# Stick-breaking queries and keys projected right behind the values, their scores and chain beside the other projection units

## The chip, the cores and the metric

The kernel runs on one core of a Trainium2 chip. The metric is the device time of one execution, in microseconds (us). Engines: PE (TensorE, matmuls), DVE (VectorE), ACT (ScalarE), POOL (GpSimd), SP (SyncE, which issues the DMAs here).

## The reference

Two transformer-like blocks of two layers each work on 256 tokens of width 1024, in float32. The change touches the first block, which runs twice (layers 0 and 1). Cut to what matters:

```
h = rms(x, ln1) * (1 + sc1) + sh1
qa,ka,va,qi,ki,wi,qb,kb,vb,qc,kc,vc = split(h @ w_in)
oa = dsa(rope(rms(qa)), rope(rms(ka)), va, rope(qi), rope(ki), wi)    # index scores, top 64 keys of each query, softmax
ob = stick_breaking(qb, kb, vb)      # no norm, no rope: z = q.k/8, log-sigmoids, reverse cumulative sum, exp
oc = window_softmax(rope(rms(qc)), rope(rms(kc)), vc, sinks)          # 8 heads in two groups, c0 and c1
x += g1 * (rms([oa, ob, oc]) @ w_o)
x += g2 * swiglu(rms(x) ...)
```

There are four heads each in the groups a, b, c0 and c1. Queries come in two blocks of 128 (n = 0 with 128 keys, n = 1 with 256 keys), so a group is two tiles.

## The kernel before, in words

**Units.** Weights stream in as units of 128 output columns (two DMAs of 256 KB). Each float32 weight is split: ACT writes the high part WH (L2158), DVE the low part of the first half (L2419, `split_low`) and POOL that of the second half (L1763, `low`); a unit is then 24 matmuls (L1846 to L1848). Four units are in flight: behind unit x every engine prepares unit x + 4, and ACT may overwrite WH only when unit x is done. Each engine works through one fixed program order and meets the others by semaphores; nothing is reordered.

**The projection** has 20 units: 0 to 3 (index queries, index keys, one key of c), 4 to 7 (values, as two pairs), then 8 to 19. Before: 8 a key of c, 9 the key of a, 10 to 13 queries of c, 14 and 15 queries of a, 16 and 17 queries of b, 18 and 19 keys of b. ACT evicts each unit from PSUM into F (L2259; with gain and a square for the normed ones, L2252 and L2257). Beside the units, PE sums squares over heads (`key_sums` L1955, `query_sums` L1965), rotates for rope (`rotate` L1982, bank 4 of PSUM) and computes index scores. `rotate(r)` of r > 0 waits until DVE has read rotation r - 1 out of bank 4 (`rot_read`); rotations of keys also wait for `k_normed`, which DVE's `key_norm` gives (four instructions, L2434, L2436, L2440, L2586). DVE ends a rope with L2575 (reads bank 4) and L2578 (adds POOL's cosine part, L1756). DVE's `highest` (L2616, L2620) takes the next 8 maxima of the index scores; 8 of them and `select` (L2627, L2631) give the top 64.

**The attention stage** runs from the last unit to the output projection. For a tile, PE computes scores (`score`: mask L2049, scores L2053), DVE its maxima (`begin`, L2687), ACT the exponentials (`exps`, L2279); PE transposes the weights (`turn`, L2069), ACT copies them (`turned_copy`, L2308 for n = 0, L2311 for n = 1), PE multiplies by the values (`weigh`, L2081), and ACT takes the heads out (`heads_out`, L2321 and L2322). The tiles go in the order of TILES: c0 0, b 0, c0 1, b 1, c1 0, c1 1, a 0, a 1. The score of a 0 waits for `select`. The b tiles have a chain of their own: `stick_begin` (DVE L2666), `stick_logs` (ACT L2288, L2290, L2292), `stick_sums` (DVE L2674, four scans L2678, L2681), `stick_exps` (ACT L2297). In the attention stage PE also multiplies the conditioning vector by streamed weights (`modulate`, L1827, 1 MB of `mods` a step, a ring of two steps); steps 5 to 15 stand between the tiles. At the end PE transposes the outputs (L2113).

Of the kernel before, what the change touches and what calls it, by code (L numbers as in the profile page):

```python
# [46 lines left out]
KEY_I, VALUES, QUERY_C, QUERY_A = 2, 4, 10, 14  # L47
KEYS = (3, 8, 9)
GAIN_OF = {3: 7, 8: 7, 9: 2, **{QUERY_C + i: 3 for i in range(4)}, QUERY_A: 0, QUERY_A + 1: 0}
ROPES = ((0, 2), (2, 1), (3, 2), (6, 2), (8, 2), (5, 1), (10, 2))  # L50
KEY_ROPES = {2: 1, 5: 2}
HEADS = {"c0": (6, 3, 1, 4, 0), "c1": (8, 4, 2, 6, 64), "a": (10, 5, 0, 0, 128), "b": (12, 14, 3, 2, 256)}
# [90 lines left out]
def build(nc, stream, mods, consts, consts2, par1, par2, lam, ccols, xT, ctxT, outT):  # L143
# [1598 lines left out]
    def _(pool):  # L1742
# [63 lines left out]
    def _(pe):  # L1806
# [109 lines left out]
        def first_layer(l):  # L1916
# [29 lines left out]
            def key_sums(c):  # L1946

                for x in KEYS[2:] if c else KEYS[:2]:
                    evicted(pe, base + x)
                if c:  # L1950
                    pe.wait_ge(mr_done, 2 * l + 1)
                else:
                    pe.wait_ge(rot_read, 7 * l + 2)
                cut = slice(2, 3) if c else slice(0, 2)
                pe.matmul(PS[:, 4, 0:(2 - c) * T], heads, SQK[:, cut, :], start=True, stop=True).then_inc(ms_done, 1)  # L1955

            def query_sums(chunks):

                for x in chunks:
                    i = x - QUERY_A if x >= QUERY_A else x - QUERY_C + 2  # L1960
                    evicted(pe, base + x)
                    pe.wait_ge(index_read, 2 * l + 2)
# [7 lines left out]
            def rotate(r):  # L1970
# [9 lines left out]
                if r in (2, 3, 4):  # L1980
                    pe.wait_ge(mr_done, 2 * l + 2)
# [13 lines left out]

            steps = iter(range(at + (NORM_STEPS if l else 0), at + QK_STEPS))
            for x in range(IN_UNITS):
# [6 lines left out]
                if x == 2:  # L2004
                    if l == 0:
                        pe.wait_ge(consts_in, 16)
                    rotate(0)
                if x == 5:
                    rotate(1)
# [16 lines left out]

            def score(i):

                name, n = SCORED[i]
                w = P * (n + 1)  # L2030
                first, key = HEADS[name][:2]
                if i < 2:
                    for x in range(16, 20):
                        evicted(pe, base + x)
                elif i < 4:
                    pe.wait_ge(stick_read, 2 * l + i - 1)
                else:
                    pe.wait_ge(exped, 6 * l + i - 3)
                if name == "c0":
                    pe.wait_ge(rope_done, 7 * l + 4)  # L2040
                if name == "c1":
                    pe.wait_ge(rope_done, 7 * l + 5)
                if name == "a":
                    pe.wait_ge(rope_done, 7 * l + 7)
                    pe.wait_ge(sel_done, l + 1)
                if name != "b":
                    m = (SELB if name == "a" else BAND)[:, n, 0:w][:, None, :].broadcast_to([P, 2, w])
                    for half in range(2):
                        pe.matmul(banks(n)[:, 2 * half:2 * half + 2, 0:w], IDB, m, start=True, stop=False)  # L2049
                for p, h in enumerate(PLACE):  # L2050
                    r = slice(64 * (h % 2), 64 * (h % 2) + 64)
                    k = key + h // 2 if name == "b" else key
                    last = pe.matmul(banks(n)[:, p, 0:w], F[r, first + h // 2, n * P:(n + 1) * P], F[r, k, 0:w],  # L2053
                                     start=name == "b", stop=name == "b" or p % 2 == 1)
                last.then_inc(scores, 1)
# [94 lines left out]
    def _(act):  # L2150
# [82 lines left out]
        def first_layer(l):  # L2233
            base = l * PER
            norm(l, 0)
            def key_roots(c):

                cut, n = slice(2, 3) if c else slice(0, 2), 2 - c
# [3 lines left out]
                             (mr_done, 2 * l + c + 1), rx_done)  # L2242

            for x in range(IN_UNITS):
# [18 lines left out]
                if x == 11:  # L2263
                    key_roots(1)
            act.wait_ge(stats_done, l + 1)
# [18 lines left out]
            def stick_logs(n):  # L2284

# [729 lines left out]
```

## Time and profile before

| | |
|---|---|
| time, 3 runs | 2315.23, 2323.94, 2323.98 us; median 2323.94 |
| span of the profiled execution | 2314.6 us |
| granted TensorE clock, mean over the span | 0.986 |
| PE, DVE, ACT, POOL busy | 96%, 56%, 48%, 33% |
| DMA | 328.47 MB, mean 142 GB/s |

The times of the three runs don't say which of them was profiled; the span lies 0.6 us under the lowest of them and 9.3 us under the median. The mean shares run over stages with different limits, so the stages around the change are read by themselves. Times of rows are from the start of the span; a number in brackets is the engine's idle time before the row and what ended it.

### The profile page before, as it was taken

The page shows a single profiled execution, that of the slowest core. Times are in us where ns is not written, and L with a number is a line of the kernel's source. Part 1 is how long each engine was busy: PE and PEld are TensorE (multiplying, and loading weights), DVE is VectorE, ACT ScalarE, POOL GpSimd, SP SyncE. Part 2 cuts the span into 40 slices and gives each one's busy share as a digit, 9 for nine tenths or more (in the row PEclk, how much of TensorE's full clock was granted, in tenths as well). Part 3 has the DMA queues.
Part 4 walks back from the last instruction along what each step waited for, and adds up shares of the span by engine and source line. Part 5 has one row for each costly group of instructions (what it writes and reads, how often), then busy time and mean ns, then how long its engine had stood idle before and what let it go on. Part 6 is the DMA issues. An engine that isn't in the chain of part 4 may idle for free.

```text
span 2314.6 us, 41122 instructions
## 1 busy us (share of the span) xinstructions
PE 2220.9 (96%) x14780; PEld 1935.8 (84%) x14780; DVE 1304.0 (56%) x2274; ACT 1112.3 (48%) x2324; POOL 764.9 (33%) x563
## 2 busy tenths in 40 slices
PE   7989998989999899999999999999989999999998
PEld 4859997868999798878878679888879999787998
DVE  3668999666445725541253764364455564437663
ACT  3565554554555535532364653232343565647553
POOL 2405874513565221112222012222213235221443
PEclk9999999999999999999999999999999999999999
DMA  8766998667766331222222113222323335222554
GB/s 303 230 219 208 322 315 301 201 210 241 237 186 196 96 91 57 64 73 91 82 74 83 35 36 94 91 73 91 99 73 110 105 116 171 83 83 65 170 162 140
DMA packets 159781, 328.47 MB, mean 142 GB/s; under 512 B 17696, under 2 KB 21024, under 8 KB 159520
## 3 DMA queue, kind: packets, MB, share of 16 engines
q1 hardware_dynamic: 159504, 325.80, 43.8%
q8 instruction: 89, 1.46, 0.2%
q0 software_dynamic: 144, 0.85, 0.1%
q14 instruction: 44, 0.36, 0.0%
HBM read 325.53 MB, written 1.05 MB: 141 GB/s over the span
## 4 chain that ended last, share of the span: by engine, by line
PE 65%; issue 14%; DVE 9%; POOL 5%; DMA 2%; ACT 2%; SPq 1%; POOLq 0%; ACTq 0%; DVEq 0%
PE PS L1846 13%; PE PS L1847 13%; PE PS L1848 13%; PE PS L1891 4%; PE PS L1893 4%; PE PS L1892 4%; POOL WL L1763 4%; DVE WORK L2521 3%; DVE WL L2419 2%; PE PS L729 2%; PE PS L709 1%; DMA RAW<-stream 1%; POOL AR L1783 1%; PE PS L743 1%; DMA WORK<-mods 1%
## 5 line engine op out<-in xcount | busy, mean ns | idle before, releaser
L1763 POOL TENSOR_TENSOR WL<-RAW,WH 128x512 fp32r<-128x512 f32 x434 | 618.7, 1427 | 1447.9 <-ACT WH L2158 1298.0
L1846 PE MATMUL PS<-AR,WH 128*128 128x256 f32 (+1 forms) x2632 | 857.9, 326 | 3.4 <-DVE AR L1614 1.9
L1847 PE MATMUL PS<-AR,WH 128*128 128x256 f32 (+1 forms) x2632 | 844.1, 321 | 0.0
L1848 PE MATMUL PS<-AR,WL 128*128 128x256 f32 (+1 forms) x2632 | 844.0, 321 | 0.0
L2158 ACT ACTIVATE WH<-RAW 128x512 fp32r<-128x512 f32 x840 | 490.6, 626 | 302.5 <-PE PS L1848 190.6
L2419 DVE TENSOR_TENSOR WL<-RAW,WH 128x512 fp32r<-128x512 f32 x434 | 372.5, 858 | 448.9 <-ACT WH L2158 447.2
L1846 PEld LDWEIGHTS PS<-AR,WH 128*128 128x128 f32 x2632 | 496.8, 189 | 58.8 <-issue 12.1
L1847 PEld LDWEIGHTS PS<-AR,WH 128*128 128x128 f32 x2632 | 496.8, 189 | 41.4 <-issue 2.4
L1848 PEld LDWEIGHTS PS<-AR,WL 128*128 128x128 f32 x2632 | 496.5, 189 | 40.1
L1891 PE MATMUL PS<-WH,AR 128*128 128x256 f32 x768 | 219.2, 285 | 0.0
L1893 PE MATMUL PS<-WH,AR 128*128 128x256 f32 x768 | 216.3, 282 | 0.0
L1892 PE MATMUL PS<-WL,AR 128*128 128x256 f32 x768 | 216.3, 282 | 0.0
L1891 PEld LDWEIGHTS PS<-WH,AR 128*128 128x128 f32 x768 | 144.7, 188 | 3.3 <-issue 3.0
L1892 PEld LDWEIGHTS PS<-WL,AR 128*128 128x128 f32 x768 | 144.7, 188 | 0.7 <-issue 0.5
L1893 PEld LDWEIGHTS PS<-WH,AR 128*128 128x128 f32 x768 | 144.6, 188 | 0.0
L1908 PE MATMUL PS<-AR,WH 128*128 128x256 f32 x352 | 99.9, 284 | 2.7 <-DVE WL L2419 2.4
L1909 PE MATMUL PS<-AR,WH 128*128 128x256 f32 x352 | 99.1, 282 | 0.0
L1910 PE MATMUL PS<-AR,WL 128*128 128x256 f32 x352 | 99.1, 282 | 0.0
L2521 DVE SCALAR_TENSOR_TENSOR WORK<-WORK 128x1024 f32<-128x1024 f32 x48 | 88.9, 1852 | 0.0
L1030 ACT ACTIVATE WORK<-PS 128x512 f32<-128x512 f32 (+1 forms) x48 | 23.5, 490 | 125.6 <-PE PS L1848 125.5
L1092 ACT ACTIVATE WORK<-PS,BC,QN 128x512 f32<-128x512 f32 (+1 forms) x96 | 66.9, 705 | 8.9 <-DVE BC L1490 8.8
L1488 DVE TENSOR_REDUCE BC<-PS 128x2 f32<-128x1024 f32 (+1 forms) x48 | 50.1, 1044 | 36.0 <-PE PS L709 36.0
(310 smaller groups left out, 3103.0 us busy)
## 6 DMA issues: line engine op xcount, KB each, us to landing
RAW<-stream SPq DMA_DIRECT2D x868, 256.0 KB, 3.0
WORK<-mods SPq DMA_DIRECT2D x144, 512.0 KB, 5.8
WORK<-stream SPq DMA_DIRECT2D x68, 256.0 KB, 4.7
C<-consts SPq DMA_DIRECT2D x1, 1088.0 KB, 7.4
XX<-xT SPq DMA_DIRECT2D x1, 1024.0 KB, 9.8
XX<-ctxT SPq DMA_DIRECT2D x1, 1024.0 KB, 7.7
outT<-XX SPq DMA_DIRECT2D x1, 1024.0 KB, 4.8
C<-consts POOLq DMA_DIRECT2D x1, 832.0 KB, 7.0
```

What stands on the lines that cost most here:

```text
L1763: pool.tensor_tensor(WL[:, u % 4, cut, :], raw(u, 1), WH[:, u % 4, cut, :].bitcast(f32), ALU.subtract).then_inc(lo_done[1], 1)
L1846: pe.matmul(out, WH[:, u % 4, k, :], moving[:, 0, k, :], start=(k == 0), stop=False)
L1847: pe.matmul(out, WH[:, u % 4, k, :], moving[:, 1, k, :], start=False, stop=False)
L1848: last = pe.matmul(out, WL[:, u % 4, k, :], moving[:, 0, k, :], start=False, stop=(k == KC - 1))
L1891: pe.matmul(out, still[:, 0, k, cut], WH[:, both, k, :], start=(k == 0), stop=False)
L1892: pe.matmul(out, still[:, 0, k, cut], WL[:, both, k, :], start=False, stop=False)
L1893: last = pe.matmul(out, still[:, 1, k, cut], WH[:, both, k, :], start=False, stop=(k == KC - 1))
L1908: pe.matmul(PS[:, b, 0:T], WH[:, u % 4, k, :], HID[:, 0, kk, :], start=(kk == 0), stop=False)
L1909: pe.matmul(PS[:, b, 0:T], WH[:, u % 4, k, :], HID[:, 1, kk, :], start=False, stop=False)
L2158: act.activation(WH[:, u % 4, cut, :], raw(u, half), ACT.Copy).then_inc(hi_done, 1)
L2419: dve.tensor_tensor(WL[:, u % 4, cut, :], raw(u, 0), WH[:, u % 4, cut, :].bitcast(f32), ALU.subtract).then_inc(lo_done[0], 1)
L2521: dve.scalar_tensor_tensor(UNREAD, GFLAT[:, h % 4, :], 1.0, CB, ALU.mult, ALU.mult, accum_out=M1[:, 1, n:n + 1]).then_inc(mod_read, 1)
```

## The change

The units of the projection are put in another order: the key of a comes as unit 3, the queries of b as 8 and 9, its keys as 10 and 11, the keys of c as 12 and 13, the queries of c as 14 to 17, those of a as 18 and 19. With them move, on each engine:

- PE: `score` of b 0 and b 1 go behind units 12 and 14 and write into the banks of the index scores (INDEX, banks 5 and 6). `key_sums(0)` and its rotation take one chunk (the key of a), `key_sums(1)` two, behind unit 14 instead of 10. The rotations 2 to 5 stand behind units 12, 16, 17 and 18; the fourth (behind 17) is now the one of the two keys of c, which waits for `key_norm(1)`. The four sums of c's queries go behind unit 18; sums and rotation of a's queries behind unit 19 and one `modulate`.
- DVE: `highest` twice instead of four times beside the units; `stick_begin(0)` at 13, `stick_begin(1)` and `stick_sums(0)` at 15, `key_norm(1)` with two chunks and a rope at 16, a rope and `stick_sums(1)` at 17. Six `highest` follow in the attention stage, where four did.
- ACT: `stick_logs(0)`, `key_roots(1)`, `stick_logs(1)` and `stick_exps(0)` behind the units 14 to 17, `stick_exps(1)` first thing in the attention stage.
- POOL: the cosine parts of the ropes follow the same order; the last one comes behind the low part of unit 23.
- The tiles go b 0, b 1, c0 0, c0 1, c1 0, c1 1, a 0, a 1; `score(3)` and two `modulate` steps move in between.

```diff
-KEYS = (3, 8, 9)
-ROPES = ((0, 2), (2, 1), (3, 2), (6, 2), (8, 2), (5, 1), (10, 2))
-KEY_ROPES = {2: 1, 5: 2}
+KEYS = (3, 12, 13)
+ROPES = ((0, 2), (2, 1), (3, 1), (10, 2), (8, 2), (12, 2), (14, 2))
+KEY_ROPES = {2: 1, 4: 2}
+ROTATED_AFTER = {2: 0, 5: 1, 12: 2, 16: 3, 17: 4, 18: 5, 19: 6}
-TILES = [("c0", 0), ("b", 0), ("c0", 1), ("b", 1), ("c1", 0), ("c1", 1), ("a", 0), ("a", 1)]
+TILES = [("b", 0), ("b", 1), ("c0", 0), ("c0", 1), ("c1", 0), ("c1", 1), ("a", 0), ("a", 1)]
...
-                for r, after in enumerate((1, 4, 11, 13, 15, 17, 18)):
+                for r, after in enumerate((1, 4, 11, 15, 16, 17, 19)):
                     if x == after:
                         cosine(l, r)
...
+                place = INDEX if name == "b" else banks(n)
+                if i == 0:
+                    for x in range(STICK, STICK + 4):
+                        evicted(pe, base + x)
+                    pe.wait_ge(index_read, 2 * l + 2)
+                elif i == 1:
+                    pe.wait_ge(stick_read, 2 * l + 1)
...
+                if x in ROTATED_AFTER and x < 19:
+                    rotate(ROTATED_AFTER[x])
                 if x == 7:
                     index_scores(0)
                 if x == 9:
                     key_sums(0)
                     index_scores(1)
-                if x == 10:
+                if x in (12, 14):
+                    score(x // 2 - 6)
+                if x == 14:
                     key_sums(1)
-                if x in (12, 14, 16, 18, 19):
-                    rotate({12: 2, 14: 3, 16: 4, 18: 5, 19: 6}[x])
-                if x == 15:
+                if x == 18:
                     query_sums(range(QUERY_C, QUERY_C + 4))
-                if x == 17:
-                    query_sums((QUERY_A, QUERY_A + 1))
...
             pe.wait_ge(band_done, 1)
-            score(0)
-            score(1)
             modulate(next(steps))
+            query_sums((QUERY_A, QUERY_A + 1))
+            rotate(6)
             score(2)
-            score(3)
             pe.wait_ge(rot_read, 7 * (l + 1))
             pe.wait_ge(qs_read, l + 1)
-            for s in steps:
-                modulate(s)
             for i in range(8):
                 turn(i)
-                if i in (0, 2, 4, 5):
-                    score({0: 4, 2: 5, 4: 6, 5: 7}[i])
+                if i == 0:
+                    score(3)
+                    modulate(next(steps))
+                if 2 <= i < 6:
+                    score(i + 2)
                 if i:
                     weigh(i - 1)
+                if i == 1:
+                    modulate(next(steps))
                 if i > 1:
                     modulate(at + i - 2)
...
+                if x == 14:
+                    stick_logs(0)
+                if x == 15:
                     key_roots(1)
+                if x == 16:
+                    stick_logs(1)
+                if x == 17:
+                    stick_exps(0)
...
+                if x == 12:
+                    rope(2)
                 if x == 13:
+                    stick_begin(0)
+                if x in (12, 13):
+                    highest()
+                if x == 15:
+                    stick_begin(1)
+                    stick_sums(0)
+                if x == 16:
                     key_norm(1)
-                if x in (12, 14, 16, 18, 19):
-                    rope({12: 2, 14: 3, 16: 4, 18: 5, 19: 6}[x])
-                if x in (13, 15, 16, 17):
-                    highest()
+                    rope(3)
+                if x == 17:
+                    rope(4)
+                    stick_sums(1)
+                if x in (18, 19):
+                    rope(x - 13)
```

## Rows read from the trace of the kernel before

**Rows 1.** Page, part 1: busy time of each engine over the span.
```profile
PE 2220.9 (96%) x14780; PEld 1935.8 (84%) x14780; DVE 1304.0 (56%) x2274; ACT 1112.3 (48%) x2324; POOL 764.9 (33%) x563
```
**Rows 2.** Windows: stretch, length, busy PE, PEld, DVE, ACT, POOL, clock, DMA, GB/s.
```profile
78.00:100.00 22.00, 21.52 (x167) 18.35 (x165) 17.83 (x26) 11.82 (x27) 10.36 (x7) 1.00 0.59 194
100.00:117.00 17.00, 17.00 (x135) 15.08 (x138) 11.79 (x30) 6.88 (x17) 9.93 (x8) 1.00 0.60 187
117.00:143.00 26.00, 19.41 (x127) 12.32 (x119) 21.20 (x64) 18.18 (x52) 0.00 (x0) 0.80 0.50 176
143.00:166.00 23.00, 21.62 (x168) 13.26 (x166) 9.62 (x30) 12.36 (x36) 0.00 (x0) 1.00 0.84 285
475.00:500.00 25.00, 18.44 (x115) 11.40 (x111) 20.03 (x60) 17.40 (x48) 0.00 (x0) 0.80 0.48 172
```
**Rows 3.** Timeline of PE, layer 0, b scores, score of a 0, output transposes.
```profile
114.93 1.68 PE L2053 MATMUL PS<-WORK 64*128 64x128 f32 x16
...
144.76 0.38 PE L2049 MATMUL PS<-WORK 128*128 128x256 bf16 x2
...
166.41 2.42 PE L2113 MATMUL PS<-C,WORK 128*128 128x128 f32 x16
```
**Rows 4.** Timeline of ACT, layer 0: evictions of units 15 to 19, stick-breaking exponentials.
```profile
98.79 0.47 ACT L2252 ACTIVATE WORK<-PS,P 128x256 f32<-128x256 f32 x1 [1.92 <-PE PS L1848]
...
103.43 0.38 ACT L2259 ACTIVATE WORK<-PS 128x256 f32<-128x256 f32 x1 [2.86 <-PE PS L1848]
...
107.15 0.38 ACT L2259 ACTIVATE WORK<-PS 128x256 f32<-128x256 f32 x1 [2.29 <-PE PS L1848]
...
110.89 0.38 ACT L2259 ACTIVATE WORK<-PS 128x256 f32<-128x256 f32 x1 [2.33 <-PE PS L1848]
...
114.18 0.38 ACT L2259 ACTIVATE WORK<-PS 128x256 f32<-128x256 f32 x1 [1.86 <-PE PS L1848]
...
132.34 1.06 ACT L2297 ACTIVATE XX<-WORK 128x1024 f32<-128x1024 f32 x1 [3.81 <-DVE WORK L2681]
```
**Rows 5.** Timeline of DVE, layer 0: stick-breaking work, top-k rounds, select.
```profile
117.42 1.81 DVE L2666 SCALAR_TENSOR_TENSOR WORK<-PS,C 128x512 f32<-128x512 f32 x2
...
122.93 0.43 DVE L2674 TENSOR_SCALAR WORK<-WORK 128x512 f32<-128x512 f32 x1
...
124.87 0.69 DVE L2681 TENSOR_TENSOR WORK<-WORK 128x512 f32<-128x512 f32 x1
...
127.82 0.68 DVE L2674 TENSOR_SCALAR WORK<-WORK 128x1024 f32<-128x1024 f32 x1
...
131.08 1.22 DVE L2681 TENSOR_TENSOR WORK<-WORK 128x1024 f32<-128x1024 f32 x1
...
138.69 1.23 DVE L2687 TENSOR_REDUCE COL<-PS 128x4 f32<-128x1024 f32 x1 [3.61 <-PE PS L2053]
...
140.42 0.61 DVE L2616 MAX8 WORK<-WORK 128x8 f32<-128x128 f32 x2
...
143.75 0.63 DVE L2631 TENSOR_TENSOR WORK<-WORK,C 128x128 bf16<-128x128 f32 x2
```
**Rows 6.** Timeline of DVE: instructions of a two-chunk key norm, in both layers.
```profile
84.49 1.76 DVE L2440 SCALAR_TENSOR_TENSOR WORK<-WORK 128x512 f32<-128x512 f32 x1
...
442.16 0.69 DVE L2440 SCALAR_TENSOR_TENSOR WORK<-WORK 128x512 f32<-128x512 f32 x1
```
**Rows 7.** Timeline of POOL, layer 0: a low part, a two-chunk cosine part.
```profile
84.41 1.29 POOL L1763 TENSOR_TENSOR WL<-RAW,WH 128x512 fp32r<-128x512 f32 x1 [0.51 <-ACT WH L2158]
...
113.64 1.46 POOL L1756 TENSOR_TENSOR WORK<-WORK,C 128x512 f32<-128x512 f32 x1
```
**Rows 8.** Windows of 2 us, columns as in Rows 2: PE thin and the clock after it.
```profile
392.00:394.00 2.00, 0.33 (x2) 0.30 (x2) 1.92 (x3) 0.05 (x1) 1.24 (x1) 1.00 0.91 306
394.00:396.00 2.00, 1.99 (x8) 0.70 (x10) 0.69 (x1) 1.73 (x4) 0.51 (x1) 0.53 0.37 138
396.00:398.00 2.00, 2.00 (x16) 0.39 (x8) 1.27 (x3) 0.57 (x2) 0.76 (x1) 0.61 0.00 0
```

More of the change, by code:

```diff
@@ L1946, in key_sums @@
             def key_sums(c):
-                for x in KEYS[2:] if c else KEYS[:2]:
+                for x in KEYS[1:] if c else KEYS[:1]:
                     evicted(pe, base + x)
[L1950 to L1955, printed above, removed]
+                pe.wait_ge(rot_read, 7 * l + 2 + c)
+                cut = slice(1, 3) if c else slice(0, 1)
+                pe.matmul(PS[:, 4, 0:(1 + c) * T], heads, SQK[:, cut, :], start=True, stop=True).then_inc(ms_done, 1)
             def query_sums(chunks):
@@ L1994, in index_scores, with score @@
                 last.then_inc(index_done, 1)
+            def score(i):
+                name, n = SCORED[i]
+                w = P * (n + 1)
+                first, key = HEADS[name][:2]
+                place = INDEX if name == "b" else banks(n)
[5 more added lines that the diff above has]
+                    pe.wait_ge(stick_read, 2 * l + 1)
+                elif i < 4:
+                    for x in (16, 17) if i == 2 else (18, 19):
+                        evicted(pe, base + x)
+                else:
+                    pe.wait_ge(exped, 6 * l + i - 3)
+                if name == "c0":
+                    pe.wait_ge(rope_done, 7 * l + 5)
+                if name == "c1":
+                    pe.wait_ge(rope_done, 7 * l + 6)
+                if name == "a":
+                    pe.wait_ge(rope_done, 7 * l + 7)
+                    pe.wait_ge(sel_done, l + 1)
+                if name != "b":
+                    m = (SELB if name == "a" else BAND)[:, n, 0:w][:, None, :].broadcast_to([P, 2, w])
+                    for half in range(2):
+                        pe.matmul(place[:, 2 * half:2 * half + 2, 0:w], IDB, m, start=True, stop=False)
+                for p, h in enumerate(PLACE):
+                    r = slice(64 * (h % 2), 64 * (h % 2) + 64)
+                    k = key + h // 2 if name == "b" else key
+                    last = pe.matmul(place[:, p, 0:w], F[r, first + h // 2, n * P:(n + 1) * P], F[r, k, 0:w],
+                                     start=name == "b", stop=name == "b" or p % 2 == 1)
+                last.then_inc(scores, 1)
             steps = iter(range(at + (NORM_STEPS if l else 0), at + QK_STEPS))
@@ L2003, in first_layer @@
                     unit(x)
[L2004 to L2009, printed above, removed]
+                if x == 2 and l == 0:
+                    pe.wait_ge(consts_in, 16)
+                if x in ROTATED_AFTER and x < 19:
+                    rotate(ROTATED_AFTER[x])
                 if x == 7:
@@ L2025, in first_layer @@
             at += QK_STEPS
[L2027 to L2055, printed above, removed]
             def turn(i):
@@ L2242, in key_roots, with stick_logs, stick_exps @@
                              (mr_done, 2 * l + c + 1), rx_done)
+            def stick_logs(n):
+                dst = PRX[n][:, :, 0:P * (n + 1)]
+                act.wait_ge(stick_read, 2 * l + n + 1)
+                chain(act.activation(dst, SM[:, n, :, 0:P * (n + 1)], ACT.Abs))
+                chain.wait()
+                chain(act.activation(dst, dst, ACT.Exp, scale=-1.0))
+                chain.wait()
+                act.activation(dst, dst, ACT.Ln, bias=EPSC[:, 1:2]).then_inc(bl, 1)
+            def stick_exps(n):
+                act.wait_ge(bq, 2 * l + n + 1)
+                act.activation(PRX[n][:, :, 0:P * (n + 1)], SM[:, n, :, 0:P * (n + 1)], ACT.Exp).then_inc(sticks, 1)
             for x in range(IN_UNITS):
@@ L2303, in turned_copy @@
                 act.wait_ge(turned, 8 * l + i + 1)
+                if i == 0:
+                    act.wait_ge(rope_done, 7 * (l + 1))
                 if i >= 4:
@@ L2637, in first_layer, with stick_begin, stick_sums @@
                 dve.tensor_copy(IDB, ident).then_inc(band_done, 1)
+            def stick_begin(n):
+                w = P * (n + 1)
+                m = strict[:, n, 0:w][:, None, :].broadcast_to([P, 4, w])
+                dve.wait_ge(scores, 8 * l + n + 1)
+                dve.scalar_tensor_tensor(SM[:, n, :, 0:w], INDEX[:, :, 0:w], 0.125, m, ALU.mult,
+                                         ALU.add).then_inc(stick_read, 1)
+            def stick_sums(n):
+                w, logs = P * (n + 1), PRX[n]
+                dve.wait_ge(stick_read, 2 * l + n + 1)
+                dve.wait_ge(bq, 2 * l + n)
+                chain(dve.tensor_scalar(STK[:, :, 0:w], SM[:, n, :, 0:w], 0.0, None, ALU.max))
+                dve.wait_ge(bl, 2 * l + n + 1)
+                chain.wait()
+                for h in range(4):
+                    chain(dve.tensor_tensor_scan(STK[:, h, 0:w][:, ::-1], logs[:, h, 0:w][:, ::-1],
+                                                 STK[:, h, 0:w][:, ::-1], 0.0, ALU.add, ALU.add))
+                chain.wait()
+                dve.tensor_tensor(SM[:, n, :, 0:w], SM[:, n, :, 0:w], STK[:, :, 0:w], ALU.subtract).then_inc(bq, 1)
             for x in range(IN_UNITS):
@@ L2721, in heads_sum @@
                                   ALU.add).then_inc(o_summed, 1)
-            stick_begin(0)
-            stick_begin(1)
             dve.wait_ge(qs_done, l + 1)
@@ L2731, in first_layer @@
             begin("c0", 1)
-            stick_sums(0)
+            highest()
             extract(group)
+            end("c0", 0)
             highest()
-            stick_sums(1)
-            end("c0", 0)
             begin("c1", 0)
+            end("c0", 1)
             highest()
-            end("c0", 1)
             begin("c1", 1)
+            highest()
             highest()
```

67 lines of the change are left out of this document (17 added, 50 removed).

## The prediction

> **What bounds the kernel now.** I read the page first: PE is busy for 96% of the span [rows 1], so outside of stages with gaps only less PE work would help, and this change keeps every matmul. The windows show where gaps are. Beside the units PE has none to speak of (21.52 of 22 us, then 17.00 of 17), while DVE has 17.83 of 22 and 11.79 of 17 [rows 2]. The attention stage is different: in 117 to 143 PE is busy 19.41 of 26 us at a mean clock of 0.80, and DVE 21.20; in layer 1 it is 18.44 of 25, again at 0.80 [rows 2]. In 143 to 166 PE is full again (21.62 of 23). So the change can gain only in the first half of the attention stage, some 25 us a layer, and what it adds beside the units meets a full PE.
>
> Then the timelines, engine by engine. ACT stands 3.81 us before the exponentials of b 1, waiting for DVE's sums [rows 4], and all later tiles queue behind them; that is the wait the change is aimed at. But DVE itself is the busier queue there: it goes from the last rope through the two stick sums and four top-k rounds to `select`, which ends at 144.38 [rows 5], and PE begins the score of a 0 at 144.76, the output transposes at 166.41, 21.65 us later [rows 3]. Layer 1 repeats this with the same gaps. What I have to find is therefore when `select` ends after the change, for the stage behind it is the same instructions in the same order.
>
> **The units, costs.** From ACT's evictions: unit 18 to 19 takes 3.29 us with a rotation of one chunk between, 16 to 17 takes 3.72 with two [rows 4]. So a chunk is 0.43 and a unit 2.86. 17 to 18 takes 3.74 with the sums of two query chunks (0.88), 15 to 16 takes 4.64 with those of four (1.78) [rows 4]. The two b scores take 1.68 [rows 3]; apart I take 0.7 and 1.1.
>
> **Before unit 15.** Key sums and rotation carry one chunk less behind 9 and 12, and key sums leave unit 10: 3 x 0.43 = 1.29 earlier. The first b score (0.7) stands where PE today waits half a microsecond for a key norm, which is shorter now: near 0. Behind unit 14 the second b score (1.1), two chunks of sums (0.86) and some 0.5 of waiting for `stick_begin(0)` replace a rotation (0.86): 1.6 later. Unit 15's eviction moves from 98.79 [rows 4] to about 99.2.
>
> **The wait behind unit 17.** PE then does unit 16, rotation 3 and unit 17: 2.86 + 0.86 + 2.86, less 0.2 by which an eviction follows PE, so it stands at rotation 4 at 105.6. Rotation 4 is of the keys of c and needs `key_norm(1)` and DVE's read of rotation 3. DVE, from 99.2: it waits 1.4 until ACT has evicted unit 15 (0.75) and written half of WH (0.6); its low part 0.6; `stick_begin(1)` 1.15 of the pair's 1.81; `stick_sums(0)` 2.6 (122.93 to the end of 124.87) [rows 5]; low part 0.6; key norm; PSUM read of the rope 0.7. For the two-chunk norm there are two prices for one and the same instruction: 0.69 us where POOL is still, 1.76 where a POOL instruction of 1.29 began just before it [rows 6, 7]. Four instructions cost 2.8 alone; I take 3.6, since a low part and a cosine part of POOL fall close by; with POOL in the way of most, 4.9. Sum 1.4 + 0.6 + 1.15 + 2.6 + 0.6 + 3.6 + 0.7 = 10.65, that is 109.8: PE stands 4.2 us (3.4 with no contention, 5.6 with much).
>
> The Trainium skill (GPSIMD Engine Reference, the table of the engine's properties) says that GpSimd's SBUF interfaces are shared with VectorE, with contention for DVE instructions with two SBUF inputs. The trace agrees, 1.76 against 0.69. By the rule alone one can't tell how long; were every moved two-input instruction to wait for a POOL one, the stall would be 5.6.
>
> **From there to the attention stage.** Rotation 4, unit 18, rotation 5, four sums and unit 19 are 0.86 + 2.86 + 0.86 + 1.78 + 2.86 = 9.2, so unit 19's eviction begins at 119.2, 5.0 later than 114.18 [rows 4]. DVE meanwhile: rest of rope 3 with POOL's cosine part (1.46, [rows 7]) beside it 1.4; low part 0.8; rope 4 1.9; `stick_sums(1)` 4.5 (127.82 to the end of 131.08) [rows 5]; low part and rope 5 2.1: 120.6. It was the queue with room, now it is late too, so the PE stall is mostly in the shadow of DVE's own work. Then `modulate`, sums and rotation of a's queries are 2.8 on PE, DVE reads rotation 6 at 122.7; the cosine part ends at 124.0, since it stands behind POOL's low part of unit 23 (121.2 + 1.3 + 1.46) [rows 7]; rope done 124.7.
>
> **To `select`.** Query roots 0.9; `begin` c0 0 1.2 and c0 1 1.75 (138.69 to 140.42) [rows 5]: 128.5. Two rounds of top-k at 1.4, `extract` 1.0, an `end` 0.2: 132.5. `begin` c1 0 1.2, an `end` and a round 1.6: 135.3. The score of c1 1 is out on PE at about 135.9 (two turns, a weigh and a step lie ahead of it, and they wait for ACT by turns); `begin` 1.75, three rounds 4.3, `select` 1.05: 143.0. Before it was 144.38 [rows 5]. So 1.4 us a layer are won; the 3.81 us of ACT's wait go, but most of them into the 4.4 us that DVE now stands idle behind unit 14, where its next low part waits for unit 15, with stick work queued behind it.
>
> **The clock.** PE has done with turn 4 at about 138.5 and then stands until 143.0. Where PE was nearly idle (0.33 of 2 us), the next two windows were granted 0.53 and 0.61 of the clock, and then it was full again [rows 8]. That is the 1.2 GHz level for most of 3.5 us, a loss of 2 x (0.47 + 0.39) = 1.7 us of work. Before, the clock is full when the score of a 0 begins, at 1.00 over 143 to 166 [rows 2], and nearly all of that stretch is PE work, so 1.6 of it counts. The stall behind unit 17 is as long and could cost the same again, as unit 18 and 19 set when DVE gets rotation 6. I charge one fall a layer of the two (bounds 0 and 3.2).
>
> The Trainium skill (TensorE: Matmul & The Clock Gate, the part on oscillation) warns of idle gaps of PE between matmuls as what brings the lower clock back. The trace agrees by 0.53 behind a gap. It speaks against this change, which makes one long gap where there was work.
>
> **Costed at nothing.** ACT's logs and exponentials beside the units: about 6 us more in stretches with 11.82 of 22 and 6.88 of 17 busy [rows 2]; without that cover evictions would be late and each would cost its length. The low parts of units 20 to 23, late on DVE by up to 7 us, are read only after 166, but raw data and `mods` of SP's queue stand behind them: steps 6 and 7 wait for step 5, now used at 120.2, and land before they are used. The steps 10 to 15, which stream at 285 GB/s near the end [rows 2], are asked for no later relative to their use.
>
> **Sum.** Per layer -1.4 + 1.6 = +0.2, both layers +0.4: 2324 us beside the median of 2323.94 (on the span 2314.6 it would be 2315.0, which is 9 under the median like before).
>
> **Rivals.**
> - *The likeliest: the wait is moved, not removed.* 2324, own range 2319 to 2330. Chance 0.55.
> - *DVE's walk without the clock falls and with little contention.* Then each layer wins 1.4, and up to 1 of contention and 0.5 of step data that arrives ahead: 3 to 6 us in all, 2319. For it: every price was taken in the middle. Against: the 4 us gaps. Chance 0.16.
> - *The overlap works in full.* `key_norm(1)` is there in time and PE, no longer DVE, sets the stage: gaps of 26 - 19.41 = 6.6 us a layer go [rows 2], and 1 of lost clock: 15 in both, 2309. It needs DVE's list before rotation 4 to be under 6.4 us where I count 10.65. Chance 0.13.
> - *Slower: rotation 4 decides.* If the stall passes 5 us and the clock falls behind it as well as before the score of a 0, the layer has +1.4 of contention and +3.2 of clock against -1.4, and unit 19 later means each `begin` later: 3.2 to 6 a layer, 2333. It decides from a stall of about 4.5 with a fall. Chance 0.16.
>
> A measurement of this kernel can tell about 0.5%, 11.6 us, from no change. Faster by more takes the full overlap, some 0.10 of its 0.13, and 0.04 of the second case: 0.14. Slower by more takes the worst of the last case: 0.09. The rest, 0.77, is within. The range: 2311 to 2334 holds all but the outer parts of the two outer cases. It is also wide by the three runs' own 8.8 us.
>
> **What the changed profile would show.** A wait of PE at the rotation of the two keys of c (L1982 before) for DVE's key norm, 3.4 to 5.6 us, once a layer; it is the first step to check. DVE idle some 4 us before the low part behind unit 14. No wait of ACT for stick sums. Top-k rounds back to back before `select`, with PE waiting for it 3 to 5 us and a granted clock near 0.5 in the windows around. `select` 1 to 3 us earlier than before, counted from the start of unit 8. The forecast is wrong if PE does not stop at rotation 4 (then faster), or if unit 19 ends more than 7 us later (then slower).

## The result: 0.58% slower, and the profile after

| | before | after |
|---|---|---|
| median, 7 runs each | 2320.62 us | 2333.00 us |
| lowest to highest | 2315.23 to 2324.93 | 2329.41 to 2336.97 |
| ratio, with its 95% interval | | 1.0058, 1.0044 to 1.0071 |
| span of the profiled execution | 2314.6 us | 2331.2 us (time 2333.0) |
| granted clock, mean over the span | 0.986 | 0.982 |

The kernel became 12.4 us slower by the medians and 16.6 us by the two profiled spans (the one of before lies low among its runs). The forecast was 2324, no change; 2333.0 lies within its range, and in the case to which it gave 0.16.

Page, part 1 of after, beside [rows 1]: PE has the same 14780 matmuls and is "busy" 10.3 us longer. That alone says that matmuls ran slower, for none was added.

```profile
PE 2231.2 (96%) x14780; PEld 1942.7 (83%) x14780; DVE 1309.9 (56%) x2274; ACT 1112.3 (48%) x2324; POOL 768.7 (33%) x563
```

The windows of after, the columns as in [rows 2], which has the same four stretches:

```profile
78.00:100.00 22.00, 21.01 (x164) 17.35 (x163) 15.55 (x29) 10.50 (x22) 8.15 (x6) 1.00 0.64 210
100.00:117.00 17.00, 11.93 (x70) 10.24 (x69) 15.50 (x20) 10.43 (x19) 8.86 (x6) 0.80 0.31 97
117.00:143.00 26.00, 25.45 (x199) 17.44 (x197) 20.19 (x57) 16.64 (x51) 4.30 (x3) 1.00 0.71 241
143.00:166.00 23.00, 18.29 (x116) 12.69 (x115) 9.27 (x34) 10.53 (x34) 0.00 (x0) 0.78 0.44 145
```

The stretch with gaps and a low clock, 117 to 143 before, is now full, 25.45 of 26 at 1.00. In its place there are two: 100 to 117 (11.93 of 17, clock 0.80) and 143 to 166 (18.29 of 23, clock 0.78), both full at 1.00 before. The first lies beside units, where DVE is the busier queue (15.50 of 17); behind the gap in the second, PE has work without a break and the other engines wait for it.

PE's timeline in after (layer 0, then three rows of layer 1) names both gaps. L1980 is `rotate`, L2068 `turn`, L2021 the mask of `score`, L2114 the output transposes:

```profile
111.39 2.05 PE L1980 MATMUL PS<-WORK,C 128*128 128x512 f32 x2 [5.07 <-DVE WORK L2581]
...
142.47 0.66 PE L2068 MATMUL PS<-C,WORK 128*128 128x128 f32 x4
...
147.84 0.58 PE L2021 MATMUL PS<-WORK 128*128 128x256 bf16 x2 [4.71 <-DVE WORK L2637]
...
174.08 2.49 PE L2114 MATMUL PS<-C,WORK 128*128 128x128 f32 x16
...
477.24 2.04 PE L1980 MATMUL PS<-WORK,C 128*128 128x512 f32 x2 [5.08 <-DVE WORK L2581]
...
513.41 0.58 PE L2021 MATMUL PS<-WORK 128*128 128x256 bf16 x2 [4.71 <-DVE WORK L2637]
...
539.34 2.49 PE L2114 MATMUL PS<-C,WORK 128*128 128x128 f32 x16 [0.18 <-DVE WORK L2790]
```

The gap before rotation 4 (L1980) is 5.07 us, the one for `select` (L2637) 4.71, and layer 1 repeats both to 0.01 us. Between the score of a 0 and the output transposes there are now 174.08 - 147.84 = 26.24 us where [rows 3] had 21.65. So layer 0 is 7.67 us behind at the transposes: 3.08 of it because the score begins later, 4.59 because the same instructions take longer.

Windows of 2 us around the two gaps, same kernel and columns:

```profile
110.00:112.00 2.00, 0.61 (x1) 0.50 (x2) 1.97 (x3) 0.56 (x2) 1.28 (x2) 0.50 0.35 132
112.00:114.00 2.00, 2.00 (x6) 1.11 (x5) 2.00 (x2) 0.00 (x0) 2.00 (x2) 0.50 0.04 8
...
116.00:118.00 2.00, 2.00 (x13) 1.78 (x13) 1.90 (x4) 0.21 (x1) 0.00 (x0) 0.85 0.93 272
...
146.00:148.00 2.00, 0.16 (x1) 0.14 (x2) 1.93 (x9) 0.00 (x0) 0.00 (x0) 0.83 0.52 213
148.00:150.00 2.00, 2.00 (x13) 1.43 (x11) 0.71 (x4) 0.00 (x0) 0.00 (x0) 0.50 0.04 8
...
156.00:158.00 2.00, 2.00 (x9) 1.15 (x9) 0.00 (x0) 1.01 (x1) 0.00 (x0) 0.61 0.81 254
```

PE is busy 2.00 of 2 but gets through 13 matmuls in a window (the windows of other kernels below show 18 and 21 there): 0.50 is the 1.2 GHz level, held from the gap to about 157. Over 143 to 166 the mean of 0.78 makes 0.22 x 23 / 0.5 = 10.1 us at half clock; PE works in all but the first half microsecond of them, some 9.6 us, which is an estimated 4.8 us of work lost. That accounts for the 4.59. ACT and DVE are idle for more than half of this stretch (10.53 and 9.27 of 23 busy), so they hide next to nothing of it.

### The profile page after: what moved, and what is told of

The parts are those of the page before. It is cut to its first block, busy times and chain, and to the rows that moved or that the text cites. A ratio compares the mean times of both kernels' runs of the same rounds, so it can differ in the third digit from the quotient of the medians.

```text
span 2331.2 us, 41120 instructions
## 1 busy us (share of the span) xinstructions
PE 2231.2 (96%) x14780; PEld 1942.7 (83%) x14780; DVE 1309.9 (56%) x2274; ACT 1112.3 (48%) x2324; POOL 768.7 (33%) x563
## 4 chain that ended last, share of the span: by engine, by line
PE 65%; issue 14%; DVE 10%; POOL 5%; ACT 2%; DMA 2%; SPq 1%; POOLq 0%; ACTq 0%; DVEq 0%
PE PS L1847 13%; PE PS L1848 13%; PE PS L1849 13%; PE PS L1892 4%; PE PS L1894 4%; PE PS L1893 4%; POOL WL L1764 4%; DVE WORK L2527 3%; DVE WL L2425 2%; PE PS L730 2%; PE PS L710 1%; DMA RAW<-stream 1%; POOL AR L1784 1%; DMA WORK<-mods 1%; PE PS L744 1%
## 5 line engine op out<-in xcount | busy, mean ns | idle before, releaser
L2425 DVE TENSOR_TENSOR WL<-RAW,WH 128x512 fp32r<-128x512 f32 x434 | 379.7, 875 | 447.7 <-ACT WH L2159 446.3
```

The source lines that it names most:

```text
L2425: dve.tensor_tensor(WL[:, u % 4, cut, :], raw(u, 0), WH[:, u % 4, cut, :].bitcast(f32), ALU.subtract).then_inc(lo_done[0], 1)
```

## The experiments

Each ratio is to runs of before on the same chip: experiments 1 to 4 shared one chip (before: 2318.17), 5 to 8 another (2318.61), 9 and 10 a third (2318.91). Kernels from different groups are therefore better compared by their ratios than by their medians. Times of rows are of layer 0 unless said. Two executions can differ before their edits begin: ACT's first eviction behind 70 us starts between 70.15 and 72.12 in the twelve kernels, so a difference of less than 2 us between the times of two kernels is weak evidence. Gaps and durations within one kernel are not touched by that.

**1. Fill the first gap** (fill17): after, with 40 matmuls whose result nobody reads, in a free bank, in front of rotation 4.

```diff
+                if x == 17:
+                    pe.wait_ge(bank_read[2], earlier(base + 18))
+                    fill(2, 40)      # 40 times 128x256, f32
                 if x in ROTATED_AFTER and x < 19:
```

> Adds 40 matmuls of 128x256 (results unused, bank 2 before unit 18 overwrites it) behind unit 17, where PE stood 5.07 us, so PE is busy there and everything else is as in the changed kernel. Theory 'clock' (a gap of 5 us costs its length once and then again by the lower clock behind it): the clock stays at 1.00 over units 18 and 19, unit 18 ends about 2.5 us earlier, select 1 to 2.5 us earlier a layer, total 2 to 5 us below the changed kernel. Theory 'queue' (DVE's late queue sets select and the clock does not matter): unit 18 may be earlier, but select moves by less than 0.7 us and the total by less than 1.5.

2332.22 us, ratio 1.0057 (1.0044 to 1.0071). PE's timeline of this kernel (L2025 is the mask of the score, L2121 the transposes):

```profile
110.97 1.10 PE L1980 MATMUL PS<-WORK,C 128*128 128x512 f32 x2 [0.28 <-DVE WORK L2588]
...
145.91 0.59 PE L2025 MATMUL PS<-WORK 128*128 128x256 bf16 x2 [4.72 <-DVE WORK L2644]
...
172.42 2.41 PE L2121 MATMUL PS<-C,WORK 128*128 128x128 f32 x16
```

The gap is filled, the clock stays at 1.00 from it to 146, and the score of a 0 comes 1.9 us earlier. The second gap is unchanged, and so is what follows it (26.51 us). The transposes of layer 0 are 1.7 us earlier, those of layer 1 0.8; the medians differ by 0.8 us, and the ratios by next to nothing (1.0058 and 1.0057). So the first gap, with its clock, is worth less than 2 us a layer.

**2. Fill the second gap** (fillsel): after, with 36 such matmuls in front of the wait for `select`.

```diff
                     pe.wait_ge(rope_done, 7 * l + 7)
+                    if n == 0:
+                        fill(0, 36)
                     pe.wait_ge(sel_done, l + 1)
```

> Adds 36 matmuls of 128x256 (results unused, bank 0 before the score of a 0 overwrites it) where PE stood 4.71 us for select. Theory 'clock': the stretch from the score of a 0 to the output transposes falls from 26.2 us to about 21.9, as it was before the change (21.65), in each layer: 8 to 9 us below the changed kernel. Theory 'queue': PE was not the limit behind select, the stretch stays above 25 us and the total moves by less than 2.

2327.21 us, ratio 1.0041 (1.0027 to 1.0055). PE's timeline (L2027 the mask, L2120 the transposes), then three windows:

```profile
146.40 0.39 PE L2027 MATMUL PS<-WORK 128*128 128x256 bf16 x2 [0.32 <-DVE WORK L2643]
...
168.38 2.42 PE L2120 MATMUL PS<-C,WORK 128*128 128x128 f32 x16
```

```profile
112.00:114.00 2.00, 2.00 (x8) 1.48 (x7) 2.00 (x3) 0.00 (x0) 2.00 (x2) 0.50 0.00 0
114.00:116.00 2.00, 2.00 (x18) 2.00 (x18) 1.97 (x3) 0.00 (x0) 0.98 (x1) 0.98 0.55 162
...
148.00:150.00 2.00, 2.00 (x21) 1.40 (x20) 0.83 (x4) 0.59 (x3) 0.00 (x0) 1.00 0.00 0
```

The same instructions behind the same `select` take 168.38 - 146.40 = 21.98 us, at a clock of 1.00, where after took 26.24. Only useless work was added, PE still begins when `select` is done, and 4.3 us come back: what the stretch behind `select` loses is the clock. The later `select` itself is the other part of the loss, and stays. By the rule of the Trainium skill (TensorE: Matmul & The Clock Gate, the part on oscillation) that idle gaps between matmuls bring the lower clock back, work in the gap should keep the clock up; the trace agrees, 1.00 against 0.50. The median gains 5.8 us (by the ratios, 1.0058 to 1.0041, about 4) where the profiled span gains 9.2. The windows also show that the low clock behind the first gap lasted to 114 here and to over 116 in after, behind gaps of the same length.

**3. Stick work earlier on DVE** (early): `stick_begin(1)` and `stick_sums(0)` behind unit 14 and not 15.

```diff
-                if x == 15:
+                if x == 14:
                     stick_begin(1)
                     stick_sums(0)
```

> stick_begin(1) and stick_sums(0) go from behind unit 15 to behind unit 14, into the 4.52 us in which DVE stood idle. Theory 'queue': key_norm(1) is ready 3.5 to 4 us earlier, the wait behind unit 17 falls from 5.07 to 1 to 2 us, select comes 3.5 to 4.5 us earlier a layer, total 7 to 9 below the changed kernel, still with PE idle before select and the lower clock behind it. Theory 'clock' agrees on the wait and adds that no fall follows unit 17, so unit 19 is 6 us earlier; select then 4.5 to 6 us earlier and the total 9 to 12 below. A third, that contention with POOL eats what the gap gives: select less than 2 us earlier, total less than 4 below.

2330.03 us, ratio 1.0050 (1.0035 to 1.0064). Two rows, the first of PE, the second of DVE:

```profile
108.76 2.04 PE L1980 MATMUL PS<-WORK,C 128*128 128x512 f32 x2 [3.68 <-DVE WORK L2581]
...
103.43 0.69 DVE L2425 TENSOR_TENSOR WL<-RAW,WH 128x512 fp32r<-128x512 f32 x1 [2.87 <-ACT WH L2159]
```

The gap shrank by 1.4 and not by the 3 to 4 expected: DVE now finishes the sums early and stands 2.87 us for ACT's high part of unit 20, with the key norm queued behind. The clock still falls in both places, the score of a 0 is at 145.30 with 4.72 of waiting, and the stretch behind it is 26.2. A shorter first gap buys little, as in 1. The total is the one of the third expectation, less than 4 us below the changed kernel, though contention is only a part of its reason.

**4. Half of the top-k rounds out of the way** (top14): three of the six rounds in the attention stage go behind unit 14, where DVE was idle 4.52 us.

```diff
+                if x == 14:
+                    for _ in range(3):
+                        highest()
...
             begin("c1", 1)
-            highest()
-            highest()
-            highest()
             select()
```

> Three of the six top-k rounds of the attention stage go behind unit 14, into DVE's idle 4.52 us (3 x 1.4 = 4.2); the wait behind unit 17 stays at 5 us. Theory 'queue': select 4.2 us earlier a layer, PE's wait for it shrinks from 4.71 to about 0.5, total 8 to 9 below the changed kernel. Theory 'clock': with that gap gone no fall follows it, the stretch behind is 21.9 instead of 26.2 us, so 8 to 9 us a layer and 16 to 18 in all, which would be below the kernel before.

2317.22 us, ratio 0.9995 (0.9984 to 1.0006): the whole loss is gone. PE's timeline and a window:

```profile
111.89 2.04 PE L1980 MATMUL PS<-WORK,C 128*128 128x512 f32 x2 [5.67 <-DVE WORK L2581]
...
143.85 0.38 PE L2021 MATMUL PS<-WORK 128*128 128x256 bf16 x2 [0.40 <-DVE WORK L2637]
...
165.65 2.42 PE L2114 MATMUL PS<-C,WORK 128*128 128x128 f32 x16
```

```profile
148.00:150.00 2.00, 2.00 (x18) 1.46 (x16) 0.00 (x0) 2.00 (x7) 0.00 (x0) 1.00 0.46 137
```

By the ratios this is 14.6 us below the changed kernel, where theory 'clock' had 16 to 18 and theory 'queue' 8 to 9. The first gap is even longer than in after, 5.67, with a clock of 0.50 from 110 to 116, unit 19 is evicted at 123.61 (after: 123.29), and yet the kernel is as fast as before. So neither the gap behind unit 17 nor the stick-breaking work beside the units costs the 12 us; the wait for `select` and the clock behind it do. The stretch from the score of a 0 to the transposes is back at 21.8 us.

**5. The one part alone** (before_top2): the kernel before, with two of its four top-k rounds taken from beside units 16 and 17 and put right ahead of `select`. Nothing else of the change is in it.

```diff
-                if x in (13, 15, 16, 17):
+                if x in (13, 15):
                     highest()
...
             begin("c1", 1)
             highest()
             highest()
+            highest()
+            highest()
             select()
```

> The kernel before with one part of the change: two top-k rounds beside the units instead of four, and six in the attention stage, of which four stand together before select. Theory 'queue and clock': select 2.8 us later a layer, PE waits some 3 us before the score of a 0, where before it came just in time; with the lower clock behind it 2.8 + 4.4 us a layer, 12 to 15 us above the kernel before. Without a fall of the clock: 5 to 6 us above. Rival, that the top-k rounds have no part in the loss: within 2 us.

2329.61 us, ratio 1.0051 (1.0037 to 1.0065): 11.0 us over before on its chip, where the change lost 12.4 and 12 to 15 were expected. PE's timeline (lines as in before) and two windows:

```profile
145.94 0.38 PE L2049 MATMUL PS<-WORK 128*128 128x256 bf16 x2 [2.25 <-DVE WORK L2631]
...
171.27 2.42 PE L2113 MATMUL PS<-C,WORK 128*128 128x128 f32 x16
```

```profile
148.00:150.00 2.00, 2.00 (x13) 1.83 (x16) 0.42 (x1) 0.15 (x1) 0.00 (x0) 0.50 0.00 0
150.00:152.00 2.00, 2.00 (x10) 0.39 (x3) 0.00 (x0) 2.00 (x9) 0.00 (x0) 0.50 0.01 4
```

The score of a 0 begins 1.2 us later than in [rows 3]. This execution was 1.7 us ahead before its edit begins (ACT evicts unit 16 at 101.71, in [rows 4] at 103.43), so the two rounds make the score 2.9 us later, which is their length of 2 x 1.4. The gap of 2.25 us was followed by a low clock, and 21.65 became 25.33. Two layers of 2.9 + 3.7 are 13.2; the profiled spans differ by 13.5 and the medians by 11.0.

**6. Key norm ahead of the low part and the sums** (norm_first): top14, with `key_norm(1)` and its rope first behind unit 16, `stick_sums(0)` after them.

```diff
             for x in range(IN_UNITS):
+                if x == 16:
+                    key_norm(1)
+                    rope(3)
                 next_low(base, 0, x)
...
                 if x == 15:
                     stick_begin(1)
-                    stick_sums(0)
                 if x == 16:
-                    key_norm(1)
-                    rope(3)
+                    stick_sums(0)
```

> Three top-k rounds behind unit 14 as before; in addition key_norm(1) and the rope behind it go ahead of DVE's low part of unit 20, and stick_sums(0) behind that. The wait behind unit 17 was 5.67 us with the three rounds alone. Theory 'order' (DVE's place for the key norm causes it): the wait falls below 1.5 us, no lower clock behind unit 17, select 2 to 4 us earlier than with the rounds alone, total 3 to 8 us below that kernel and about 0.3% under the kernel before. Rival 'gap moves': PE is early and waits at select again, 2 us or more; if the clock then falls there, 4 us a layer are lost again and the total is at or above that of the rounds alone.

2322.64 us, ratio 1.0015 (1.0006 to 1.0025), 5 us over top14 and no gain. PE's timeline:

```profile
108.63 1.37 PE L1980 MATMUL PS<-WORK,C 128*128 128x512 f32 x2 [2.96 <-DVE WORK L2581]
...
116.45 2.05 PE L1980 MATMUL PS<-WORK,C 128*128 128x512 f32 x2 [2.33 <-DVE WORK L2581]
```

One gap of 5.67 became two of 2.96 and 2.33, and the clock fell behind each: in the windows it is at 0.50 or near it from 109 to 113 and from 116 to 126. The score of a 0 is 3.2 us later than in top14. Here two short gaps cost more than a long one.

**7. Useless work where there is no gap** (norm_first_fill): 6 with 24 unused matmuls ahead of the wait for `select`, the same edit as in 2.

> The same with 24 matmuls whose results are unused (2.9 us) in PE's wait before the score of a 0. If the gap moved there and the clock fell, this is 6 to 9 us below the kernel without them; if it did not fall, it is the same or up to 3 us above.

2326.60 us, ratio 1.0032 (1.0021 to 1.0043). There was no gap (0.41 us) to fill in 6, so the fill delays the score of a 0: from 147.08 to 148.91 in layer 0 (1.3 of that is there before the edit, in ACT's first eviction behind 70 us) and from 506.01 to 510.29 in layer 1, and 4 us are lost in all. It supports that experiment 2 gained by the gap and not by anything else in such matmuls.

**8. Both at once** (top14_fill17): top14 with 44 unused matmuls before rotation 4, the edits of 4 and 1 together.

> Three top-k rounds behind unit 14 and 44 matmuls whose results are unused (5.2 us) in the wait behind unit 17: both gaps of the changed kernel covered, the work in its order. Theory 'clock': 1 to 2 us a layer below the kernel with the rounds alone, so 2 to 4 us in all. Rival: DVE sets select and nothing moves by more than 1 us.

2315.70 us, ratio 0.9985 (0.9976 to 0.9994), the fastest version that ran, 1.5 us under top14 by the medians and about 2 by the ratios (the two intervals overlap). PE's timeline:

```profile
141.33 0.38 PE L2025 MATMUL PS<-WORK 128*128 128x256 bf16 x2 [0.40 <-DVE WORK L2644]
...
163.60 2.42 PE L2121 MATMUL PS<-C,WORK 128*128 128x128 f32 x16
```

The clock is at 1.00 in all windows from 110 to 158. Layer 0 reaches its transposes 2.8 us earlier than in [rows 3] and 2.0 earlier than top14; layer 1 reaches its own 0.8 us later than top14 (522.30 beside 521.48). So even with both gaps dealt with, the time is 0.15% lower than before, and no more.

**9 and 10. Another order on PE** (unit18_top14 and unit18): top14, and after itself, with unit 18 and the sums of c's queries ahead of rotation 4, and rotation 5 behind unit 19.

```diff
-ROTATED_AFTER = {2: 0, 5: 1, 12: 2, 16: 3, 17: 4, 18: 5, 19: 6}
+ROTATED_AFTER = {2: 0, 5: 1, 12: 2, 16: 3}
...
                 if x == 18:
                     query_sums(range(QUERY_C, QUERY_C + 4))
+                    rotate(4)
+                if x == 19:
+                    rotate(5)
```

> Three top-k rounds behind unit 14; and on PE unit 18 and the four sums of c's queries (4.6 us of work) go ahead of the rotation of c's keys, so the wait behind unit 17 is covered by real work; rotation 5 goes behind unit 19. Theory 'clock and queue': the wait falls from 5.67 us to under 1, the clock stays at 1.00 from unit 15 to the attention stage, the total is 2 to 8 us under the kernel with the rounds alone and at or under the one whose gap was filled with unused matmuls, so 0.1 to 0.4% under the kernel before. Rival 'DVE sets it': select comes less than 1 us earlier than with the rounds alone, the total within 2 us of it.

> The changed kernel with the PE order alone altered (unit 18 and the four sums ahead of the rotation of c's keys), the top-k rounds left as the change has them. It undoes the first of the two gaps. Theory: no wait over 1 us behind unit 17 and no lower clock there, select 1.5 to 3 us earlier a layer; the gap before the score of a 0 stays at 4.5 to 5 us with the lower clock behind it; total 3 to 6 us below the changed kernel and still 0.2 to 0.4% over the kernel before. Rival, that the first gap is the main cause: at or under the kernel before.

2320.62 us, ratio 1.0006 (0.9994 to 1.0018; one run of 11628 us, far outside all others, is left out), and 2335.71 us, ratio 1.0076 (1.0063 to 1.0089). Both are 3 to 4 us over the kernels that they start from, where a gain had been expected. PE's timeline of unit18_top14:

```profile
112.80 1.10 PE L1980 MATMUL PS<-WORK,C 128*128 128x512 f32 x2 [1.15 <-DVE WORK L2584]
...
126.21 2.04 PE L1980 MATMUL PS<-WORK,C 128*128 128x512 f32 x2 [5.12 <-DVE WORK L2584]
```

PE's row and a window of unit18:

```profile
111.54 1.60 PE L1980 MATMUL PS<-WORK,C 128*128 128x512 f32 x2 [0.54 <-DVE WORK L2584]
```

```profile
112.00:114.00 2.00, 2.00 (x7) 1.40 (x6) 2.00 (x2) 0.40 (x1) 2.00 (x3) 0.50 0.00 0
```

The gap was moved, not filled: unit 18 covers most of rotation 4's wait, but DVE does `stick_sums(1)` before the rope that rotation 6 waits for, and PE then stands 5.12 us there. The expected gain took no account of DVE's order. That order (the rope ahead of the sums) was not tried. Nor did covering the wait keep the clock up, as expected: behind the remaining 1.15 us (unit18_top14) and 0.54 us (unit18), which come right after the sums of c's queries, it was low for some 3.4 us.

## Why the prediction was wrong

Its likeliest case, no change, was wrong; its first step was right, and its "slower" rival came nearest. By its steps:

- **Before unit 15.** Eviction forecast at 99.2, measured 99.79. Right.
- **The wait behind unit 17.** Forecast 4.2 us (3.4 to 5.6), measured 5.07; the mechanism is right. DVE's rows of after show what was off:

```profile
101.09 0.69 DVE L2425 TENSOR_TENSOR WL<-RAW,WH 128x512 fp32r<-128x512 f32 x1 [4.52 <-ACT WH L2159]
...
103.36 2.27 DVE L2661 TENSOR_TENSOR_SCAN WORK<-XX,WORK 128x128 f32<-128x128 f32 x4
105.67 1.59 DVE L2664 TENSOR_TENSOR WORK<-WORK 128x512 f32<-128x512 f32 x1
...
107.78 0.68 DVE L2440 TENSOR_TENSOR WORK<-WORK 128x512 f32<-128x512 f32 x1
...
109.22 0.69 DVE L2446 SCALAR_TENSOR_TENSOR WORK<-WORK 128x512 f32<-128x512 f32 x1
```

  I priced contention with POOL into the key norm (3.6 us) and none into the stick sums (2.6). It was the other way round: the norm ran alone (107.78 to 110.64, 2.9), the sums took 4.4 (102.83 to 107.26), their scans 2.27 and their last instruction 1.59, against 0.69 for that one in [rows 5]. Low parts and a cosine part of POOL ran beside the sums. DVE's idle time ahead of it, 4.52, was forecast as 4.4.
- **From there to the attention stage.** Unit 19 forecast at 119.2. ACT's rows of after, units 15, 18 and 19:

```profile
99.79 0.47 ACT L2268 ACTIVATE WORK<-PS,P 128x256 f32<-128x256 f32 x1 [1.69 <-PE PS L1849]
...
117.79 0.47 ACT L2268 ACTIVATE WORK<-PS,P 128x256 f32<-128x256 f32 x1 [7.24 <-PE PS L1849]
...
123.29 0.47 ACT L2268 ACTIVATE WORK<-PS,P 128x256 f32<-128x256 f32 x1 [3.71 <-PE PS L1849]
```

  Rotation 4 and unit 18 took 6.4 us and not 3.9, mostly at half clock. The clock fell behind this gap, which the likeliest case did not charge.
- **To `select`.** Forecast to end at 143.0, 1.4 under before; it ended at 147.69, 3.3 over. DVE's rows, `begin` c1 1 and `select`:

```profile
140.56 1.22 DVE L2704 TENSOR_REDUCE COL<-PS 128x4 f32<-128x1024 f32 x1 [1.71 <-PE PS L2025]
...
147.06 0.63 DVE L2637 TENSOR_TENSOR WORK<-WORK,C 128x128 bf16<-128x128 f32 x2
```

  The whole miss is there already when this `begin` starts, 140.56 where I had 135.9; what follows it took the 7.1 us forecast. Against [rows 5] the 3.3 us are 1.87 of a later `begin` (138.69 before) and 1.4 of a third top-k round behind it where there were two. Of the 4.7 us to my figure, 4.1 stand already at unit 19's eviction (123.29 beside 119.2): 0.6 from unit 15, 0.9 of longer gap and 2.5 in rotation 4 and unit 18. The last 0.6 was not taken apart. Fill17, which removes the gap and its clock, gains 1.9 at the score of a 0.
- **PE's wait for `select`.** Forecast from 138.5 to 143.0, 4.5 us; measured 4.71, from 143.13 to 147.84. The size was right. Against before, 3.1 of it are the later score and 1.6 are that PE is done earlier. There is a second cause beside the top-k rounds: the change puts the score of c1 1 behind the fourth `turn` instead of the third, so PE has 2.7 us of work between it and the score of a 0 (140.44 to 143.13) where before had 6.3 (138.48 to 144.76), and DVE stands 1.71 us for that score before its `begin`. Whether that score a tile earlier would also close the gap was not tried.
- **ACT's wait.** No stick exponential waits for DVE's sums any more, as forecast, but no gain shows: top14 has it and ends level with before. How much it gave and how much the other parts took back was not separated.
- **The clock, the step that failed.** I charged one fall a layer at 1.6 us, sized by one short stretch, [rows 8], with bounds 0 and 3.2. There were two falls: one behind rotation 4, which lengthened rotation and unit 18 by about 2.5 us and so makes more than half of the 4.7 us by which `select` missed its forecast, and one behind `select`, which cost 4.6, three times the term. So both terms of the sum failed, -1.4 (measured +3.3) and +1.6 (measured +4.6), and the clock accounts for about half of the first miss and all of the second. The kernel's own longer stretch was in front of me: 0.80 over the 26 us of 117 to 143 in [rows 2] is 0.20 x 26 / 0.5 = 10.4 us at half clock, three times what I took. I had used that row for gaps, and for 1 us of lost clock in one rival.
- **Costed at nothing.** ACT's logs and exponentials beside the units, late low parts and `mods`: top14 keeps all of them and is level with before, so they cost no more than what the change wins elsewhere. That they cost nothing is not shown.
- **The sign for slower.** "Unit 19 ends more than 7 us later" came true (9.1), but it was no sign of the loss: in top14 it is 9.4 later and nothing is lost. The sign was the clock behind `select`.

Per layer that is +3.1 for the later score and +4.6 for the clock behind it, 7.7, and 15.05 over both at the transposes of layer 1 (539.34 beside 524.29), where the sum had +0.2 a layer. The rival "rotation 4 decides" gave 2333 with its mechanism of two falls, at a chance of 0.16. Its two falls were right, and its number came true in part by luck, for its terms were others (3.2 us of clock a layer and a `select` level with before, where 4.6 and 3.3 us later came). The place that it named was wrong: the experiments put the loss at the top-k rounds ahead of `select` (before_top2 makes 11 of 12.4 us with nothing else; top14 takes all of it back while rotation 4 waits still longer), and at most 2 us a layer at rotation 4.

Did before not pay for its own low clock? It had a fall too, at 128 to 138. A row of PE and two windows of before:

```profile
134.02 1.94 PE L2069 MATMUL PS<-C,WORK 128*128 128x128 f32 x8 [2.66 <-ACT WORK L2308]
```

```profile
136.00:138.00 2.00, 2.00 (x8) 1.10 (x8) 0.00 (x0) 1.19 (x3) 0.00 (x0) 0.50 0.00 0
138.00:140.00 2.00, 2.00 (x20) 1.24 (x18) 1.28 (x2) 0.38 (x2) 0.00 (x0) 0.96 0.01 4
```

Until 134.02 PE stood much of the time for ACT and DVE, so that part of the fall was in their shadow. From there to the score of a 0 it worked without a break, and DVE stood 3.61 us for PE's score of c1 1 [rows 5]. So the last 4 us of the fall lay in PE's path, an estimated 2 us of work lost; no run kept the clock of before up, so this is not measured. Top14's fall at 110 to 116 is not hidden altogether either, for with its gap filled the score of a 0 came 2.5 us earlier in layer 0 (141.33 beside 143.85), though the whole kernel gained only some 2 us. What the change added is the fall behind `select`, at the head of a stretch that PE sets from end to end, and that one is paid in full.

**Open.** In fill17 the score of a 0 is 1.9 us earlier but the total only 0.8, and in fillsel the span gains 9.2 and the median 5.8; neither is explained (that executions already differ ahead of an edit is part of it). Why the clock stayed low behind the same 5 us gap to 114 in one kernel and past 116 in another is not either. What the order of PE's scores has in the loss was not tested by itself.

## What to carry to other kernels

Price a moved wait as the gap plus the slow clock behind it, and size that from the longest low-clock stretch that the kernel's own trace has, counting what of it PE works in, not from a short one: here gaps of 2.25 and 4.71 us ahead of a full PE stage cost 3.7 and 4.6 us more behind them. Ask first which engine sets the pace behind the gap: a fall where PE waits anyway costs little, one at the head of a full PE stage is paid in full. Removing a wait from an engine that isn't the bound gave no measurable gain here by itself, while work pushed to the end of the queue that a full stage waits for made nearly the whole loss (two top-k rounds cost 11 us in before_top2); it belongs where that queue is idle.

## What the runs showed of the hardware

- Short gaps were followed by long low clocks: 2.25 us (before_top2) by 0.50 for some 7 us, 2.96 and 2.33 us (norm_first) by some 3.5 and 10 us, and 1.15 us (unit18_top14) and 0.54 us (unit18) by some 3.4.
- Behind gaps of about 5 us PE worked at the low clock for 3 us (fillsel, first gap), 5 (after, first gap) and some 9.6 (after, behind `select`).
- Matmuls of no use in the gap kept the clock at 1.00 from 110 to 158 (top14_fill17), and where there was no gap they cost their own time (norm_first_fill).
- L2664 of `stick_sums(0)` took 1.59 us where a low part of POOL (1.48 us) had begun 0.44 us before it, and 0.69 in [rows 5]. It ended 0.55 us after POOL's. Its scans took 2.27 us in after, where a cosine part of POOL ran from 102.90 to 104.40, and 1.37 in before. By the Trainium skill (SBUF — State Buffer, the part on who interferes with whom) the later of two such instructions is blocked until the earlier is done; the trace agrees nearly: POOL's ended at 105.23 + 1.48 = 106.71, and the 0.55 us from there to 107.26 are a little less than the 0.69 that L2664 takes alone.
